# Loading each expert's two weight matrices with one long run per partition, in a two-block fused kernel on one Trainium2 core

## The reference

```
xs = t[tok_s]                                    # token rows, sorted by expert
hu = lax.ragged_dot(xs, w1, sizes)               # w_expert_in[l, e]: 1024 x 1024
h_gate, h_up = jnp.split(hu, 2, axis=-1)
ys = lax.ragged_dot(jax.nn.silu(h_gate) * h_up, w2, sizes)   # w_expert_out[l, e]: 512 x 1024
ys = ys * flat_gate[order][:, None]
out = jnp.zeros_like(t).at[tok_s].add(ys)
```

## Time and profile before

| | |
|---|---|
| median of 3 runs | 3999.5 us (3993.81 to 3999.94) |
| the profiled execution | 4006.5 us, its span 4004.8 us |
| PE busy | 3338.8 us, 83% of the span |
| DVE, ACT, POOL busy | 1182.0, 858.7, 671.3 us |
| moved by DMA | 665.18 MB, a mean of 166 GB/s |
| blocks | 66 (one gather each), in two stages of about 520 and 545 us |

### The profile page before, as it was taken

The page is one execution under the profiler, slowest core; times in us unless marked ns, Lnnn a source line. Parts: engine busy times, 40 slices in busy tenths (PEclk is TensorE's granted clock), DMA queues, the critical chain, the costliest instruction groups (busy, mean ns, idle before and its releaser), DMA issues. The chain is left out here.

```text
span 4004.8 us, 41122 instructions
## 1 busy us (share of the span) xinstructions
PE 3338.8 (83%) x14329; PEld 1956.9 (49%) x14329; DVE 1182.0 (30%) x2139; ACT 858.7 (21%) x1253; POOL 671.3 (17%) x367
## 2 busy tenths in 40 slices
PE   5796798788884796698788786788799988879999
PEld 3573364433332574364433332553488447338854
DVE  2356402211112347511211110363333015433310
ACT  0523211111111423311111111222232022323300
POOL 2311010111111221010111111300234021013300
PEclk7897898899997897799799999888899999889999
DMA  8311023799997421023699999210132322012222
GB/s 300 120 52 41 11 90 122 312 409 409 409 406 288 162 73 36 5 95 128 236 397 408 410 409 364 73 43 1 63 99 65 90 87 84 1 42 85 92 65 64
DMA packets 287753, 665.18 MB, mean 166 GB/s; under 512 B 20282, under 2 KB 110704, under 8 KB 287600
## 3 DMA queue, kind: packets, MB, share of 16 engines
q1 hardware_dynamic: 269632, 623.43, 41.8%
q0 software_dynamic: 17968, 39.73, 2.8%
HBM read 655.47 MB, written 25.44 MB: 170 GB/s over the span
## 5 line engine op out<-in xcount | busy, mean ns | idle before, releaser
L822 PE MATMUL psum<-s_parts 128*128 128x512 f32 (+3 forms) x3392 | 830.3, 398 | 112.3 <-ACT s_parts L1908 96.6
L822 PE MATMUL psum<-s_ring,s_units 128*64 128x512 f32 x3168 | 746.2, 621 | 128.7 <-DMA s_ring<-in_w_expert_in 89.9
L822 PEld LDWEIGHTS psum<-s_parts 128*128 128x128 f32 (+1 forms) x3392 | 637.6, 194 | 277.0 <-issue 99.9
L822 PEld LDWEIGHTS psum<-s_ring,s_units 128*64 128x64 f32 x3168 | 250.7, 142 | 580.8 <-issue 450.9
L822 PE MATMUL psum<-s_units,s_ring 128*128 128x512 f32 x1216 | 524.0, 593 | 3.3 <-DVE s_units L1581 3.3
L822 PE MATMUL psum<-s_units 128*128 (+9 forms) x1532 | 406.0, 450 | 128.1 <-ACT s_units L1908 52.5
L801 POOL TENSOR_TENSOR s_parts<-s_ring,s_parts 128x4096 fp32r<-128x4096 f32 x30 | 270.1, 9008 | 996.5 <-ACT s_parts L1908 996.5
L822 PEld LDWEIGHTS psum<-s_units,s_ring 128*128 128x128 f32 x1216 | 231.2, 190 | 290.5 <-issue 289.7
L822 PE MATMUL psum<-s_h_low,s_parts 128*128 128x512 f32 (+1 forms) x1440 | 355.9, 389 | 0.0
L822 PEld LDWEIGHTS psum<-s_units 64*128 64x128 f32 (+3 forms) x1532 | 206.7, 206 | 258.2 <-issue 198.2
L822 PEld LDWEIGHTS psum<-s_h_low,s_parts 128*128 128x128 f32 (+1 forms) x1440 | 269.1, 187 | 57.5
(11 more groups left out here) (313 smaller groups left out, 2425.2 us busy)
## 6 DMA issues: line engine op xcount, KB each, us to landing
s_ring<-in_w_expert_in SPq DMA_DIRECT2D x132, 2048.0 KB, 23.7
s_ring<-in_w_expert_out SPq DMA_DIRECT2D x66, 2048.0 KB, 24.8
s_ring<-in_w_in SPq DMA_DIRECT2D x28, 2048.0 KB, 7.9
s_ring<-in_w_ada SPq DMA_DIRECT2D x24, 2048.0 KB, 19.7
s_ring<-in_ffn_w_up SPq DMA_DIRECT2D x44, 1024.0 KB, 6.7
s_ring<-in_ffn_w_down SPq DMA_DIRECT2D x16, 1408.0 KB, 7.7
s_ring<-in_w_out SPq DMA_DIRECT2D x8, 2048.0 KB, 7.8
s_units<-ys_scratch POOLq DMA_DIRECT2D x16, 512.0 KB, 6.3
```

The lines of the kernel that those rows point to most:

```text
L822: return pe.matmul(o, lhsT=lhsT, rhs=rhs, start=start, stop=stop)
```

## The change

The two halves of the input matrix become one transfer of 4 MB into two neighbouring ring slots, and partition p now takes rows 8p to 8p+7 of the matrix, which lie next to each other in DRAM: one run of 32 KB per partition, where there were eight runs of 4 KB (row k*128 + p for each k). The output matrix takes rows 4p to 4p+3 in one run of 16 KB, where there were four of 4 KB. What a partition holds has changed, so three other places follow. The token rows in `h2t` are written in another order, each copy scattering its columns 128 floats apart. `gate_up` picks other columns of the weights: for each c the moving operand is every fourth float (the index q of `(h q c i)`), in four groups of 128, where it was two runs of 256 floats next to each other. And its second wait, for slot 3u+1, is gone, since both slots land with one transfer. The stationary operands and all of `down` read as before.

```diff
-            for j in range(3):
-                s = 3 * u + j
-                if layer_first:
-
-                    sp.wait_ge(TA.done.sem, TA.done_at(l, RA.reader_last(s) if s < 3 else ("gb", 7)))
+            for kind, first, slots in (("w_expert_in", 0, 2), ("w_expert_out", 2, 1)):
+                for j in range(first, first + slots):
+                    s = 3 * u + j
+                    if layer_first:
+                        sp.wait_ge(TA.done.sem, TA.done_at(l, RA.reader_last(s) if s < 3 else ("gb", 7)))
+                        settle(sp)
+                    sp.wait_ge(freed_in_m[j].sem, freed_in_m[j].at(number, u - 1))
                     settle(sp)
-
-                sp.wait_ge(freed_in_m[j].sem, freed_in_m[j].at(number, u - 1))
-                settle(sp)
-                if j < 2:
-                    sp.dma_start(slot_view(s, 4, D), kn(inp["w_expert_in"][l, e], 0, D)[:, 4 * j:4 * j + 4, :]).then_inc(weights_in_m[s], 16)
-                else:
-                    sp.dma_start(slot_view(s, 4, D), kn(inp["w_expert_out"][l, e], 0, D)).then_inc(weights_in_m[s], 16)
+                s = 3 * u + first
+                place = ring[:, s:s + slots, :].rearrange("p s n -> p (s n)")
+                sp.dma_start(place, inp[kind][l, e].rearrange("(p k) n -> p (k n)", p=P)).then_inc(weights_in_m[s], 16)
...
                     s = 3 * u + j
-                    pe.wait_ge(weights_in_m[s], pairs * 16 + 16)
                     if j == 0:
+                        pe.wait_ge(weights_in_m[s], pairs * 16 + 16)
...
-                            both = w[:, k, :].rearrange("p (h f) -> p h f", h=2)[:, :, 256 * c:256 * c + 256]
-                            last = mm(psum[half, u, :].rearrange("p (h f) -> p h f", h=2), xsT[u][:, k, CAP * j:CAP * j + CAP],
+                            both = w[:, k, :].rearrange("p (h q c i) -> p c h i q", h=2, c=2, i=2)[:, c]
+                            last = mm(psum[half, u, :].rearrange("p (h i q) -> p h i q", h=2, i=2), xsT[u][:, k, CAP * j:CAP * j + CAP],
...
-                copy(h2t[(i // 2) % 2][:, 512 * (i % 2):512 * (i % 2) + 512], o).then_inc(TA.by(("tm", i)).sem, TA.by(("tm", i)).more())
+                turned = h2t[(i // 2) % 2].rearrange("s (r k b) -> s k b r", r=8, k=KD)[:, 4 * (i % 2):4 * (i % 2) + 4]
+                copy(turned, o.rearrange("s (k b r) -> s k b r", k=4, r=8)).then_inc(TA.by(("tm", i)).sem, TA.by(("tm", i)).more())
```

## The result

The changed kernel takes 4354.0 us (median of 4 runs, 4347.49 to 4364.62), the kernel before on the same chip 3996.7 (3991.98 to 3999.94): a ratio of 1.0898, 95% interval 1.0869 to 1.0926. That is 357 us slower, against the 310 that were forecast. The profiled execution took 4348.9 us with a span of 4347.1, 342 more than before; over 66 blocks that is 5.2 us a block, so a block now takes 15.9 + 5.2 = 21.1 us.

What follows compares the result with a forecast made beforehand. Expert weight transfers set the pace at 15.9 us a block, PE close behind at 13.7. The slow operand lifts PE to 20.6, adding 310 us to 4006.5: 4316 profiled, so 4310 timed, range 3960 to 4420.

Steps and rivals of the forecast that it cites:

- the likeliest case: gate_up's spread operand slows its matmuls by a factor of 1.3 to 2.2; 4180 to 4390 us, chance 0.44.
- The operand: gate_up's moving floats 16 bytes apart cost a factor of 1.95, taking it from 7.3 to 14.2 us a block.
- no slack: In gate_up, two streams together read as many floats per ns as anything on PE, so slower reads would show.
- PE's round: PE's work per expert block grows from 13.7 to 20.6 us and sets the pace, adding 310 us.
- The transfers: Expert weights in longer runs save 0.77 us a block, 51 us over 66 blocks, hidden once PE sets the pace.
- the circle: Scatter landing, put_at, indices, down, scaling, next scatter: 13.6 us a block beside the transfers' 15.9, margin 2.3.
- The later request: Input matrix asked for after gate_up's second half, 3.65 us later than its first half was; costed at nothing.
- The copies of ACT: ACT's eight scattered copies a layer, even doubled, add 4.7 us, covered by POOL's 7.2 us idle; costed at nothing.
- A: gate_up's operand is free and the queue behaves: up to 51 us gained, say 3970 us; chance 0.22.
- B: Operand free, but long weight runs delay gathers and scatters: 17.2 us a block, 4085 us at worst; chance 0.12.
- C: Long weight runs are cut to 4 KB and gate_up's operand is free: no change, 4000 us; chance 0.06.
- D: gate_up's streams share one port, factor 3.9: 5250 us; chance 0.12 together with anything beyond a factor of 2.3.

Runs made afterwards that it cites:

- e7: Changed kernel with gate_up reading pairs of neighbouring floats, and DVE copying indices to SBUF and writing put_at after the block's multiply: 3964.2 us, ratio 0.9925.
- e9: Kernel before, with DVE copying indices to SBUF at once and writing put_at after the block's multiply: 3996.1 us, ratio 1.0006.
- e5: Changed kernel with gate_up reading pairs of neighbouring floats, down's transposes reading with stride 2 to undo the order: 4075.4 us, ratio 1.0198.
- e1: Changed kernel with gate_up's operand in plain runs and the output matrix in 4 KB runs as before: 4005.2 us, ratio 1.0029.
- e11: Changed kernel with DVE copying indices to SBUF at once and writing put_at after the block's multiply: 4342.8 us, ratio 1.0871.
- e8: Changed kernel with gate_up's loops turned, c outermost, so that matmuls of one stream follow one another: 4602.2 us, one run.

## Why the prediction was right

The forecast, its direction and its mechanism held: 4310 us forecast, 4354 measured, inside the likeliest case's own range of 4180 to 4390. Its steps one by one:

**The operand, factor 1.95.** Predicted 891 ns for a pair of records, measured 0.90 us. gate_up was put at 14.2 us and takes 14.4 to 14.6, a factor of 1.97 to 2.0 on 7.3. The number came from DVE's floats 32 bytes apart (1.74 ns each), with the choice to carry the time and not the bare factor of 1.67. The experiments show that this was no accident of one row: 16 and 32 bytes cost alike on PE (1078 and 1097 ns for the median record), and the price is a time per float and stream, 0.90 us / 512 = 1.76 ns. Part of it was luck all the same: that DVE and PE pay the same time per float was an assumption, and no row before bore it out. The reason given ("no slack") was also only half of it, since 8 bytes apart is a spread read too and costs 5%: what counts is how many floats of the same 16 bytes are read. (The working also divides 427 ns by 512 where the row quoted gives 431; nothing hangs on it.)

**PE's round, 20.6 us.** It is 20.3 in the block shown, and 21.1 in the mean by the span. This is the term that was mis-sized, and it makes up 33 us (0.5 us x 66) of the 44 between 4310 and 4354. The other 11 are in what was added to the profiled execution: it was put 6 us above the time that was forecast (4316 and 4310), and came 5 below the measured median (4348.9 and 4354.0). What the round left out is the clock. In blocks with a table load PE waits 0.91 and 0.56 us around the transposes, and after such waits down and the first of gate_up sometimes run at a low granted clock. Here it is 0.60, and the 48 records take 19.75 us and not 18.05:

```profile
908.71 0.44 PE L1160 MATMUL psum<-s_ident,s_units 128*128 128x128 f32 x2 [0.91 <-DVE s_units L1701]
909.71 19.75 PE L820 MATMUL psum<-s_ring,s_units 128*64 128x512 f32 x48 [0.56 <-issue]
```

```profile
909.71:914.00 4.29, 4.29 (x12) 1.58 (x14) 0.50 (x1) 0.00 (x0) 1.39 (x1) 0.60 1.03 443
914.00:918.00 4.00, 4.00 (x14) 1.08 (x12) 0.00 (x0) 0.69 (x1) 0.90 (x1) 1.00 1.00 429
```

After the same waits at 952.01 and 953.01 the next stretch took 18.05 us at a full clock. In the two expert stages the timeline has 57 unbroken stretches of 48 records. 41 of them take 18.05 or 18.06 us, and 16, all of them behind such waits, 19.58 to 20.63. Those 16 are 33 us longer together, which is the whole of the mis-sizing. Why the clock falls in one block and not in the other stays open.

**The transfers, 9.6 ns and 36.8 ns per KB, a gain of 0.77 us a block that stays hidden.** It did stay hidden. Its size could only be seen with the circle opened: e7 against e9 is 3964.2 against 3996.1 on the same chip, 32 us or 0.48 us a block, where 51 us were predicted. The cost of a run itself was right: 1214 ns for 32 KB and 612 for 16 KB were predicted, and the packets take 1214 and 612 ns in e7's trace. The rate rose from 409 to 427 GB/s, 4.4%, near the 5% (0.77 of 15.4 us at 409) that the two costs give; that the time follows by less goes with PE's waits for gathers, 1.9 us in 300, and I did not separate the rest. That runs are not cut is shown by the count of packets.

**The later request and the missing second wait, nothing.** Right: PE waited for no expert weights at all.

**The copies of ACT, 4.7 us under POOL's 7.2.** The row of all such copies rose from 591 to 622 ns. That is the mean of 242, of which 16 are the scattered ones. The eight of the first layer take 1070 ns in the median, where they took 594; they come in two groups of four that are busy for 3.69 and 3.78 us, 7.5 together, where all eight were busy for 4.2. So they cost 3.3 us more, less than the 4.7 that were allowed. POOL's idle time before the first gather is 5.26 us, still not zero. So it was hidden.

**The rivals.** A (a free operand, 3970) was wrong about the operand. B had the right mechanism: gathers and scatters land after 10.1 and 8.3 us, the 8 to 10 that the prediction named as its sign, and e5 and e1 show that it binds once the operand is cheap. Its price was right in the sum and not in the parts, which is luck: a circle of 17.2 us predicted, 16.9 measured in e5, but 7.3 for the landing (predicted 9.7) and 9.6 for the rest (predicted 7.5). The low clock in down is 1.7 of these 2.1. So had the operand been nearly free, as in e5, the kernel would still have been slower, and the chance of 0.22 for A beside 0.12 for B was the wrong way round. In the changed kernel B is hidden under PE's 21.1 us, which e11 shows. C is out by the packets (each 32 KB run is one), D by the 0.90 us of a pair and by e8.

## What to carry to other kernels

When a layout for longer runs spreads the operand that a matmul streams, look at the innermost stride first: keep at least two float32 of every 16 bytes in use, by choosing which columns go together (pairs of neighbours here), and the operand costs 5%; at 16 bytes its time doubles, and here that was 7.1 us a block, where the transfers had 0.5 to 0.8 to give. Before counting the gain of longer runs, list what else uses the DMA engines and who waits for it: here small gathers and scatters came up to 5 us later, and a circle with 2.3 us of margin became the pace. The remedy was to copy a result out of PSUM at once, and to do the write that waits for a transfer only after the work that others wait for. It cost one small copy a block on DVE, and turned e5, at 4075 us, into the fastest version, at 3964.

## What the runs showed of the hardware that was not expected

- The price of a spread float32 moving operand is a step, not a slope: the median record takes 593 ns for neighbours, 612 at 8 bytes and for pairs of neighbours, 1078 at 16 bytes, 1097 at 32.
- Two slow streams side by side, on the two halves of the array's columns, don't slow each other, and one alone is no faster: 0.90 us from start to start in each case, with the DMA engines busy or idle. Losing part of the overlap costs 4602 against 4354 us.
- A run of 32 KB is a single packet, and takes 1214 ns, one of 16 KB 612 and one of 4 KB 159 to 164. With 32 and 16 KB runs the 16 DMA engines move 427 GB/s against 409 with 4 KB.
- A PE wait of 1.97 us was followed by 3.3 us at a granted clock of 0.62 (e5), and waits of 0.91 and 0.56 us by 4.3 us at 0.60 in one block and by a full clock in another (changed kernel). There it made 16 of 57 stretches of matmuls 1.5 to 2.6 us longer.
